# A chunked RWKV-7 recurrence: from chunks of 32 tokens with head pairs to chunks of 64 with single heads

## The reference

```
state = state * w_t + (state @ a_t) outer b_t + v_t outer k_t      # 64 x 64 per head
y_t   = state @ r_t                                                # then normed per head, + bonus, * gate
out   = x + rms_norm(concat(y, pool) @ w_out);  out += rms_norm(conv_ffn(rms_norm(out)))
```

## Time and profile before

| | |
|---|---|
| time of the runs, median (lowest to highest) | 2328.89 us (2323.8 to 2330.03), 3 runs |
| the profiled execution, span | 2329.1 us |
| granted TensorE clock, mean | 0.987 |
| PE, DVE, ACT, POOL busy | 96%, 75%, 49%, 44% |
| the recurrence's first instruction | 548.7 us |
| last copy of y in the recurrence | 841.0 us |

### The profile page before, as it was taken

How to read it: one execution, slowest core, us unless ns; L and a number is a source line. 1 busy time by engine, 2 the same in 40 slices (tenths; PEclk the granted TensorE clock), 3 DMA queues, 4 the chain that set the end, 5 groups by cost and what they waited for, 6 DMA issues and landing times.

```text
span 2329.1 us, 43634 instructions
## 1 busy us (share of the span) xinstructions
PE 2231.0 (96%) x16652; PEld 1816.6 (78%) x16652; DVE 1756.5 (75%) x1910; ACT 1141.8 (49%) x1795; POOL 1025.4 (44%) x726
## 2 busy tenths in 40 slices
PE   7999999996999979998999999999999999999998
PEld 6777777775878768887888888788788888887886
DVE  3756798994884466769989999666799898976565
ACT  5646556452445554444444444454554444444543
POOL 4636466571234335535776766100146555541000
PEclk9999999998999989999999999999999999999999
DMA  7364556347567547895434343677733332326774
GB/s 203 93 227 134 178 160 209 106 140 216 154 166 194 144 144 234 268 279 166 153 119 147 121 146 128 217 252 255 237 119 115 104 111 93 113 95 202 247 260 145
DMA packets 435819, 395.61 MB, mean 170 GB/s; under 512 B 59548, under 2 KB 352076, under 8 KB 432332
## 3 DMA queue, kind: packets, MB, share of 16 engines
q1 hardware_dynamic: 407804, 343.06, 47.8%
q10 hardware_dynamic: 27856, 50.34, 6.0%
HBM read 266.97 MB, written 126.35 MB: 169 GB/s over the span
## 4 chain that ended last, share of the span: by engine, by line
PE 55%; DVE 3%; DMA 2%; ACT 1%; issue 1%; SPq 0%; ACTq 0%; POOLq 0%; POOL 0%; DVEq 0%
PE late_bank L133 18%; PE late_bank L134 18%; PE late_bank L135 18%; DVE wt_lo L2906 1%; DMA scratch_a<-p_keep 1%; ACT wt_hi L2727 1%; PE late_bank L2199 1%; DMA o_lo<-scratch_q 0%; DVE wt_lo L2860 0%; DMA p_keep<-in_w_down 0%; DMA raw<-in_w_down 0%; DMA scratch_x<-x_tile 0%; DMA p_keep<-scratch_td 0%; DVE p_ub L2869 0%; DVE x_tile L2168 0%
## 5 line engine op out<-in xcount | busy, mean ns | idle before, releaser
L133 PE MATMUL late_bank<-o_hi,wt_hi 128*128 128x512 f32 x1232 | 481.3, 391 | 8.0 <-DVE o_lo L2962 3.3
L134 PE MATMUL late_bank<-o_lo,wt_hi 128*128 128x512 f32 x1232 | 480.7, 390 | 0.0
L135 PE MATMUL late_bank<-o_hi,wt_lo 128*128 128x512 f32 x1232 | 480.6, 390 | 0.0
L431 POOL TENSOR_TENSOR p_w_lo<-p_w_raw,p_w_hi 128x1024 fp32r<-128x1024 f32 x72 | 190.4, 2645 | 221.2 <-ACT p_w_hi L502 221.2
L133 PEld LDWEIGHTS late_bank<-o_hi,wt_hi 128*128 128x128 f32 x1232 | 232.0, 188 | 58.7 <-issue 7.2
L135 PEld LDWEIGHTS late_bank<-o_hi,wt_lo 128*128 128x128 f32 x1232 | 232.1, 188 | 48.8
L134 PEld LDWEIGHTS late_bank<-o_lo,wt_hi 128*128 128x128 f32 x1232 | 232.0, 188 | 47.8
L2597 POOL TENSOR_TENSOR tsum<-raw 128x512 f32<-128x512 f32 x43 | 106.2, 2469 | 358.5 <-DVE p_ub L2947 179.4
L133 PE MATMUL p_ppr<-p_hT_hi,p_w_hi 128*128 128x512 f32 x576 | 233.4, 405 | 0.2 <-ACT p_ring L513 0.2
L133 PE MATMUL late_bank<-wt_hi 128*128 128x512 f32 x572 | 223.2, 390 | 7.2 <-DVE wt_lo L2906 6.6
L135 PE MATMUL p_ppr<-p_hT_hi,p_w_lo 128*128 128x512 f32 x576 | 226.6, 393 | 0.0
(11 more groups left out here) (328 smaller groups left out, 4679.3 us busy)
## 6 DMA issues: line engine op xcount, KB each, us to landing
raw<-in_w_up SPq DMA_DIRECT2D x88, 512.0 KB, 5.1
p_w_raw<-in_w_in SPq DMA_DIRECT2D x72, 512.0 KB, 3.9
scratch_a<-p_keep SPq DMA_DIRECT2D x22, 1280.0 KB, 4.5
raw<-scratch_a SPq DMA_DIRECT2D x96, 256.0 KB, 3.0
raw<-scratch_td SPq DMA_DIRECT2D x52, 256.0 KB, 3.7
p_keep<-scratch_a SPq DMA_DIRECT2D x47, 256.0 KB, 2.9
scratch_a<-p_keep SPq DMA_DIRECT2D x44, 256.0 KB, 2.0
raw<-in_w_down SPq DMA_DIRECT2D x44, 256.0 KB, 4.1
```

The costliest lines, as they stand in the source:

```text
L133: nc.tensor.matmul(out, lhs_hi, rhs_hi, start=start, stop=False, skip_group_check=again)
L134: nc.tensor.matmul(out, lhs_hi, rhs_lo, start=False, stop=False, skip_group_check=again)
L135: return nc.tensor.matmul(out, lhs_lo, rhs_hi, start=False, stop=stop, skip_group_check=again)
L431: nc.gpsimd.tensor_tensor(w_lo[i][:, :, :], w_raw[i][:, :, :], w_hi[i][:, :, :].bitcast(F32), ALU.subtract).then_inc(s_wl, 1)
```

## The change

Chunks have L = 64 tokens, two per group of 128, and each head stands alone. Nothing is padded and GpSimd no longer builds `bk`: b and k of a chunk are loaded side by side, and one product per head and chunk gives the grams of both with a and r (128 x 128). from_state multiplies a with the state directly (row halves of the array for the two heads, two PSUM banks), the inverse is applied after it (`inverse`), so w and aT go, with their transposes, row copies and stores in the projection and their loads here. The inverse of 64 tokens is put together from the two of 32 and a corner: x1 transposed on VectorE, `corner_left` and `corner_right` on TensorE, with copies on ScalarE. bT and kT come from two runs of transposes in place of four, the state chain has two links of two TensorE runs (from_state, inverse) and to_state in place of four. Product calls of a turn go from 228 to 156. y's centring, square and scaling move to GpSimd (tensor_tensor), the sums and the reciprocal stay on VectorE. The solves in this phase have six gaps a turn and five turns each: turns 0 to 4 and 5 to 9. DRAM scratch holds a with r, b with k, bonus with gate side by side per group (512-byte pieces for a, r, bonus and gate in the projection's stores). y, mo and the bonus and gate tiles get one more buffer.

```diff
+        GAPS = 6
+        TURNS = 5
+        PARTS = GAPS * (TURNS - 1) + 3
...
+        TURN = {"y": 1, "m1": 0, "t0": 0, "t1": 1, "x21": 0}
...
+                    for c in range(2):
+                        sp.dma_start(x1[n % 2][:, c, :, :], upper[k, g, 0, c]).then_inc(s_xl[n % 2], 16)
+                    for c in range(2):
+                        for e in range(2):
+                            sp.dma_start(xt[g][quad(c, e), :, C * e:C * e + C], whole[k, g, c, e]).then_inc(s_xl[n % 2], 16)
+                        for h in range(2):
+                            sp.dma_start(xd[n % 2][quad(c, h), :, :], lower[k, g, 1, c, h]).then_inc(s_xl[n % 2], 16)
...
+                        gp.wait_ge(s_mean, ONE + n + 1)
+                        nc.gpsimd.tensor_tensor(y[n % 3][:, :, :], y[n % 3][:, :, :], stat[p][:, 0, :].unsqueeze(2).to_broadcast([P, HEADS, H]),
+                                                ALU.add).then_inc(s_yc, 1)
+                        if n:
+                            gp.wait_ge(s_var, ONE + n)
+                        gp.wait_ge(s_yc, ONE + n + 1)
+                        nc.gpsimd.tensor_tensor(y2[:, :, :], y[n % 3][:, :, :], y[n % 3][:, :, :], ALU.mult).then_inc(s_sq, 1)
...
+                        gp.wait_ge(s_rec, ONE + n + 1)
+                        nc.gpsimd.tensor_tensor(y[n % 3][:, :, :], y[n % 3][:, :, :], stat[p][:, 3, :].unsqueeze(2).to_broadcast([P, HEADS, H]),
+                                                ALU.mult).then_inc(s_yc2, 1)
...
+                    def take_p(c2):
+
+                        act.wait_ge(s_as, ONE + i * 2 + c2 + 1)
+                        nc.scalar.activation(pz[rows_of(c2), :, :].rearrange("s (h j) v -> s h j v", h=2), pbank[rows_of(c2)], ACT.Copy).then_inc(s_p, 1)
...
+                        take("x21", *((xt[(i + 1) % BATCH][quad(c2, 0), :, C:L],
+                                       lambda v, c2=c2: v[quad(c2, 0), 0:HEADS * C].rearrange("p (u t) -> p u t", t=C)) for c2 in range(2)))
                     if c:
                         act.wait_ge(s_var, ONE + i - 1)
-                        nc.scalar.activation(stat[:, 2, :], stat[:, 1, :], ACT.Sqrt, scale=1.0 / H, bias=geps[:, 0:1]).then_inc(s_sd, 1)
...
+                    def masked(c2):
+
+                        dve.wait_ge(s_gd, ONE + 2 * (i + 1) + c2 + 1)
+                        nc.vector.tensor_tensor(am[rows_of(1), c2, :, :].rearrange("s (h j) t -> s h j t", h=2), gbank[rows_of(1), :, :, 0, :],
+                                                strict[rows_of(1), :].unsqueeze(1).unsqueeze(1).to_broadcast([L, 2, PAIRS, L]), ALU.mult).then_inc(s_gm, 1)
+                        dve.wait_ge(s_lr, ONE + 2 * (i + 1) + c2 + 1)
+                        nc.vector.tensor_tensor(ark[(i + 1) % 3][:, c2], gbank[:, :, :, 1, :],
+                                                causal[:, :].unsqueeze(1).unsqueeze(1).to_broadcast([P, 2, PAIRS, L]), ALU.mult).then_inc(s_gm, 1)
...
+                    if c:
+                        n = i - 2
+                        dve.wait_ge(s_yr, ONE + n + 1)
+                        nc.vector.tensor_reduce(stat[p][:, 0, :], y[n % 3][:, :, :], AX.X, ALU.add).then_inc(s_gn, 1)
+                        dve.wait_ge(s_gn, ONE + n + 1)
+                        nc.vector.tensor_scalar(stat[p][:, 0, :], stat[p][:, 0, :], -1.0 / H, None, ALU.mult).then_inc(s_mean, 1)
                     if a2:
-                        masks(am[q], strict, 0, s_am)
+                        n = i + 1
+                        dve.wait_ge(s_xl[n % 2], ONE + (n // 2 + 1) * 160)
+                        if n:
+                            wait_full(dve, i - 1, "m1")
+                        nc.vector.transpose(x1u[:, :, :, :].rearrange("p c u s -> p (c u s)"), x1[n % 2][:, :, :, :].rearrange("p c u t -> p (c u t)")
+                                            ).then_inc(s_xu, 1)
                     gap(0)
+                    gap(1)
+                    if i == N - 1:
+                        low_w(0)
+                    if a2:
+                        masked(0)
                     if b:
                         advance(0)
                     if a2:
-                        masks(ark[slot], causal, C, s_gr)
-                    gap(1)
-                    if i == N - 1:
-                        low_w(0)
-                    if b:
-                        advance(1)
-                        dve.wait_ge(s_sn, ONE + i * CH + 2)
-                    if c:
-                        dve.wait_ge(s_yr, ONE + i - 1)
-                        nc.vector.tensor_reduce(stat[:, 0, :], yv, AX.X, ALU.add).then_inc(s_gn, 1)
-                        dve.wait_ge(s_gn, ONE + g + 1)
-                        nc.vector.tensor_scalar(stat[:, 0, :], stat[:, 0, :], -1.0 / H, None, ALU.mult).then_inc(s_gn, 1)
-                        dve.wait_ge(s_gn, ONE + g + 2)
-                        nc.vector.tensor_tensor(yv, yv, stat[:, 0, :].unsqueeze(2).to_broadcast([P, DBL, H]), ALU.add).then_inc(s_yc, 1)
-                    gap(2)
-                    gap(3)
+                        masked(1)
...
+                    def from_state(c2):
+
+                        pe.wait_ge(s_z, ONE + i * 2 + c2 + 1)
+                        if i * 2 + c2:
+                            pe.wait_ge(s_sn, ONE + i * 2 + c2)
+                        else:
+                            pe.wait_ge(s_xz, ONE + BATCH + 1)
+                        for j in range(PAIRS):
+                            for h in range(2):
+                                last = nc.tensor.matmul(pbank[rows_of(c2), h, j, :], ar[now][half(h), j, 0, tokens(c2)],
+                                                        st[p][c2][half(h), j, :], start=False, stop=True, skip_group_check=True)
+                        last.then_inc(s_as, 1)
+
+                    def inverse(c2):
+                        if c2 == 0:
+                            wait_read(pe, i - 1, "x21")
+                        pe.wait_ge(s_p, ONE + i * 2 + c2 + 1)
+                        for j in range(PAIRS):
+                            for h in range(2):
+                                u = h * PAIRS + j
+                                last = nc.tensor.matmul(ubank[:, h, j, :], xt[now][rows_of(c2), u, :], pz[rows_of(c2), u, :],
+                                                        start=True, stop=True, skip_group_check=True)
+                        last.then_inc(s_xp, 1)
...
+                    def grams(c2):
+
+                        if c2:
+                            pe.wait_ge(s_gm, ONE + 4 * (i + 1) + 2)
+                            pe.wait_ge(s_lr, ONE + 2 * (i + 1) + 1)
+                        else:
+                            pe.wait_ge(s_gm, ONE + 4 * (i + 1))
+                            pe.wait_ge(s_lr, ONE + 2 * (i + 1))
                         for j in range(PAIRS):
-                            for h2 in range(2):
-                                last = nc.tensor.matmul(bank[half(h2), SB, j * H:(j + 1) * H], bkt[p][:, j * CH + c4, half(h2)], now[:, c4, j, :],
-                                                        start=True, stop=True)
-                        last.then_inc(s_s, 1)
-
-
-
-                    def from_r(h2):
-                        if h2 == 0:
+                            for h in range(2):
+                                last = nc.tensor.matmul(gbank[:, h, j, :, :], kinds[half(h), j, 2 * c2:2 * c2 + 2, :].rearrange("d m s -> d (m s)"),
+                                                        ar[nxt][half(h), j, :, tokens(c2)], start=True, stop=True)
+                        last.then_inc(s_gd, 1)
...
+                                    last = nc.tensor.matmul(at[quad(c2, h), j * C:(j + 1) * C], l21[:, c2, u, :], x1u[:, c2, u, :],
...
+                                last = nc.tensor.matmul(at[quad(c2, 0), u * C:(u + 1) * C], m1[quad(c2, h), j, :], xd[q][quad(c2, h), j, :],
...
+                    if a2:
+                        pe.wait_ge(s_in[(i + 1) % 2], ONE + 80 * ((i + 1) // 2 + 1))
                     if b:
-                        wait_read(pe, i - 1, "w1")
                         from_state(0)
                     if a2:
-                        bk_transposes(0)
+                        grams(0)
                     if b:
-                        to_state(0)
+                        inverse(0)
                     if o:
                         from_r(0)
                     if d:
-                        pe.wait_ge(s_yc2, ONE + i - 2)
-                        turn("y", lambda o, j: nc.tensor.transpose(o[:, j * SC:(j + 1) * SC], y[q][:, 2 * j:2 * j + 2, :].rearrange("p h v -> p (h v)"),
-                                                                   ident[:, :]), PAIRS)
+                        turn_y()
+                    if b:
+                        to_state(0)
+                    if a2:
+                        grams(1)
+                    if o:
+                        from_r(1)
                     if b:
                         from_state(1)
```

(64 more changed lines are left out.)

676 lines of the change are left out of this document (280 added, 396 removed).

## The result

The changed kernel takes 2379.68 us in the median (2370.75 to 2388.16, 4 runs), the kernel before 2329.46 beside it (2323.8 to 2336.16, 4 runs). The ratio estimated from all runs is 1.0203, with an interval of 1.0165 to 1.024. By the medians it is slower by 50 us; 2341 was forecast, 2292 to 2360 the range. The profiled execution of the changed kernel took 2378.76 us, its span is 2376.9, 47.8 more than that of before.

What follows compares the result with a forecast made beforehand. TensorE was taken to bound the kernel, VectorE close behind during the solve. On 2329.1 us: turns 1 to 9 +29, turns 10 to 13 -11, projection -5, its end -1.7, the end +1, net +12: 2341 us, range 2292 to 2360.

Steps and rivals of the forecast that it cites:

- Transfers: DMA transfers and their issues: engines busy 12 of 14.3 us a turn, SP's issues filling 12.6 us; cost nothing.
- the 1.7 and 5 us of the projection: Projection: 5 us saved by dropping runs of 16 transposes, 1.7 at its end by halving the last stores.
- The end: After the last turn: the last y passes GpSimd's 1.3 us operations in place of VectorE's 0.7; 1 us lost.
- runs and loop: Recurrence: TensorE's priced runs sum to 14.0 us a turn; VectorE's mask loop makes it 14.3 without the solve.
- Rival E: TensorE's row halves don't overlap in from_state and grams: +11 and +12 us, 2364 us in total; chance 0.06.
- The three shares: Turns 1 to 9: three solve pieces on VectorE stand in the loop to TensorE's masks; 26 pieces, 23 us.
- the lock: Turns 1 to 9: GpSimd's tensor_tensor operations on y hold the shared ports and delay VectorE's solve steps; 15 us.
- The clock: Turns 1 to 9: after waiting for masks, TensorE does 3.3 us of work a turn at half speed; 15 us.
- Rival D: TensorE's clock stays down longer after its waits: 15 us more, 2356 us in total; chance 0.10.
- A: Turns 1 to 9: solve pieces cost as forecast, but neither port lock nor clock adds anything; 2312 us, chance 0.17.
- B: Solve pieces are absorbed too, TensorE's sum alone holding: 14.3 us in all 13 turns, 2288 us; chance 0.12.
- C: GpSimd's port lock costs as forecast but TensorE keeps full clock: 2326 us, no change; chance 0.20.

Runs made afterwards that it cites:

- experiment 2: The changed kernel with its stores of bonus, b and a, still in 512-byte pieces, issued by SyncE instead of ScalarE: 2372.59 us (1.0179).

## Why the prediction was wrong

**The step that failed** is "Transfers": "I cost them at nothing", and with it the 1.7 and 5 us of the projection. It asked whether the DMA engines have room and whether SyncE's issues fill a turn, and took an issue at 0.37 us, or twice that. It never asked how long an issue of 2048 pieces holds the engine that makes it, nor who is queued behind it: the projection's stores are ScalarE's, and TensorE waits for ScalarE at each block's start. That is 28 us by the trace, 26 by the medians, more than half of the 50. The prediction had the projection and its end as a gain of 6.7 us; they were a loss of 15.0. Of the 28.0 us, 21.7 are TensorE's longer waits at the starts of three blocks.

**The end** was costed at +1 by comparing durations (GpSimd's 1.3 us against 0.7). What counts is the queue in front: GpSimd's row holds back the last y by 4.4 us at the centring and by 5.4 at the scaling. +10.5.

**Held:** runs and loop. TensorE's turn was 13.3 us where 14.0 was summed. Rival E is out: the 16 records of from_state take 0.68 us, those of the grams 1.16. Without the solve the nine turns take 129.6 (128.7 expected), with it 50.7 more (53 expected: 23, 15 and 15). The terms of the 53 were mis-sized. The three shares cost 15.3 us of waiting for the mask where 23 was forecast, and the lock 21.8 and not 15, because a step of the solve met every one of GpSimd's five operations, the two on mix among them, which the prediction had left uncounted; together 37.1 against 38, which is luck.

**The clock** was right in kind and a little small. TensorE is busy 136.0 us with the 2700 records of the nine turns, and 119.5, 117.1 and 115.7 in the runs without the solve and with the shares moved, at clocks of 0.95 to 0.99. So the lower level costs some 17 to 20 us in the profiled execution, against the 15 forecast (the 50.7 are 37.1 of waits and 16.5 of busy time, less 2.9 of other idle time); in that of the stores from SyncE, with the same recurrence, TensorE is busy 145.4, some 26 to 30 us more than in those three runs. Rival D's clock of twice the price (30) is then within what these nine turns do in other profiled executions.

**Rivals.** A fell with the solve's steps of 1.35 us, B with the 20 us turns, C with the clock of 0.73.

**Right by luck in part:** the 11 us of the turns without a solve. They were worked out as four turns of 2.7; from the 10th to the 16th copy of y there are six. The three turns from the 10th to the 13th gained 10.0 us, the last three 3.4, which makes 13.4.

**Wrong without a price:** that the root's place behind x21 keeps VectorE from running ahead. With the shares gone from the loop it makes no difference.

**Open:** why the pieces cost 17.6 us in the kernel before and 28.0 in the changed one. The traces show where: up to the start of the fourth block they cost 16.3 and 22.4 us, in the rest of the projection 1.3 and 5.6; there runs of four records of 512 columns (L908) behind the last stores take 3.78 and 3.57 us in the changed kernel, 1.98 and 1.96 with large pieces, 1.98 and 1.88 in the kernel before with small pieces (L926), so the lower clock is part of it. Open too: whether the number of the pieces or their spacing in DRAM sets the issue's time, and why TensorE's busy time in the nine turns scatters by 9 us at equal waits.

## What to carry to other kernels

When a layout in DRAM changes, count the pieces of each store and ask what stands behind its issue on the issuing engine; a transfer that is hidden can have an issue that is not. When work is spread into the gaps of an engine's program, ask of each gap whether it lies between a neighbour's result and the mask or copy that the neighbour waits for: the same solve cost 50 us of nine turns with three shares a turn in one place and nothing with them in another. When a wait lets the clock fall, read its price from the busy time of the same records in two runs: the difference of two totals books it with whatever was taken out. For an operation moved to another engine, its place in that engine's row at the end of the phase counts, not its duration.

## What the hardware showed that was not expected

In the projection of the changed kernel the issue of a store took 0.4 to 0.6 us where no other store of its queue had started within 2 us before it, whatever the pieces (the gate's in the first block: 0.60 with pieces of 512 bytes, and 0.60 with 2048 in the run with large pieces; k's on SyncE, 2.3 us behind r's, both in 512-byte pieces: 0.55). For 2048 pieces it took 6.2 to 7.5 us on ScalarE in the third of three stores of 1 MB in a row, started 1.8 to 2.8 us behind the first; with 512 pieces 1.4 to 2.0. On SyncE, where experiment 2 put them, the three issues of the first block took 1.01, 6.80 and 3.46 us. TensorE's clock was at the lower level after waits of 3.09 and 3.64 us although 3.4 us of products stood right ahead of them, and stayed at 1.00 from 600 to 750 us where 5.6 us of products left waits for the mask of 1.4 us at most.
